# A diffusion trunk step on one core: conditioning products of 512 columns written as two of 256

## The reference

```python
def adaln(cvec, w, b):
    m = jax.nn.silu(cvec) @ w + b            # (groups, 1024) @ (1024, 6144) + (6144)
    return jnp.split(m[:, None, :], 6, axis=-1)

def trunk(x, cvec, ...):
    for l in range(DEPTH):                   # DEPTH = 2
        sh1, sc1, g1, sh2, sc2, g2 = adaln(cvec, ada_w[l], ada_b[l])
        h = rmsnorm(x, norm1_g[l]) * (1 + sc1) + sh1
        ...
        x = x + g1 * mix
        h = rmsnorm(x, norm2_g[l]) * (1 + sc2) + sh2
        ...
        x = x + g2 * ff
```

## Time and profile before

| what | value |
|---|---|
| median of 3 runs | 1561.68 us (1560.41 to 1563.05) |
| profiled execution, its own time | 1562.52 us |
| its span, first to last instruction | 1560.7 us |
| mean granted TensorE clock | 0.975 of full speed |
| TensorE (PE) busy, its weight loads (PEld) | 1496.6 us (96%), 1243.6 us (80%) |
| DVE, ACT, POOL busy | 1149.5 us (74%), 917.6 us (59%), 15.0 us (1%) |
| HBM read | 460.98 MB, 296 GB/s over the span |

### The profile page before, as it was taken

One profiled execution on the slowest core, in us unless ns is written; L12 is line 12 of the kernel. 1 busy time (PEld: TensorE's weight loads), 2 busy tenths in 40 slices (PEclk: granted clock), 3 DMA queues, 4 the chain that ended last, 5 costly groups with the idle time before them and its releaser, 6 DMA issues.

```text
span 1560.7 us, 21348 instructions
## 1 busy us (share of the span) xinstructions
PE 1496.6 (96%) x8173; PEld 1243.6 (80%) x8173; DVE 1149.5 (74%) x1054; ACT 917.6 (59%) x756; POOL 15.0 (1%) x28
## 2 busy tenths in 40 slices
PE   6999898999798999999999999999999999999997
PEld 3888796999577788888888878888888888887886
DVE  2658654555444788888888888878878888888886
ACT  1433442333313777677677677677767767766774
POOL 1000000000000000000000000000000000000000
PEclk9699999999998999999999999999999999999998
DMA  9758778655456799899899889989989989997990
GB/s 325 268 166 293 265 242 301 197 190 187 135 198 234 259 366 362 298 374 359 304 349 369 325 328 370 356 291 364 370 288 364 367 327 326 360 368 283 372 348 29
DMA packets 221825, 463.37 MB, mean 297 GB/s; under 512 B 7572, under 2 KB 48696, under 8 KB 221768
## 3 DMA queue, kind: packets, MB, share of 16 engines
q1 hardware_dynamic: 220984, 460.83, 81.8%
q0 software_dynamic: 784, 1.75, 0.5%
HBM read 460.98 MB, written 1.57 MB: 296 GB/s over the span
## 4 chain that ended last, share of the span: by engine, by line
PE 90%; DVE 3%; ACT 3%; DMA 2%; SPq 1%; issue 0%; POOL 0%; DVEq 0%; ACTq 0%
PE ps L409 87%; PE ps L790 2%; SPq L881 1%; ACT hT L978 1%; DMA raw<-in_w_in 1%; DVE w_lo L1133 1%; DMA raw<-in_fourier_w 1%; ACT w_hi L953 1%; DMA raw<-in_ffn_w 1%; DVE rstd L1208 1%; PE ps L447 0%; PE ps L487 0%; ACT arena L1090 0%; DVE xT L1366 0%; DVE hT L1212 0%
## 5 line engine op out<-in xcount | busy, mean ns | idle before, releaser
L409 PE MATMUL ps<-w_hi,rnd 128*128 128x512 f32 x2720 | 875.2, 398 | 1.6 <-DVE rnd L1442 1.6
L1448 DVE TENSOR_TENSOR w_lo<-raw,w_hi 128x2048 fp32r<-128x2048 f32 x335 | 765.3, 2290 | 144.7 <-ACT w_hi L1047 144.2
L1047 ACT ACTIVATE w_hi<-raw 128x2048 fp32r<-128x2048 f32 x336 | 644.0, 1918 | 201.8 <-PE ps L409 201.8
L409 PEld LDWEIGHTS ps<-w_hi,rnd 128*128 128x128 f32 x2720 | 511.1, 188 | 122.0 <-issue 1.8
L409 PE MATMUL ps<-w_lo,rnd 128*128 128x512 f32 x1360 | 537.6, 395 | 0.0
L409 PE MATMUL ps<-rnd,w_hi 128*128 128x256 f32 x1632 | 298.8, 286 | 8.7 <-DVE rnd L1219 6.8
L409 PEld LDWEIGHTS ps<-w_lo,rnd 128*128 128x128 f32 x1360 | 255.8, 188 | 57.9
L409 PEld LDWEIGHTS ps<-rnd,w_hi 128*128 128x128 f32 x1632 | 255.1, 193 | 16.3 <-issue 10.1
L409 PE MATMUL ps<-rnd,w_lo 128*128 128x256 f32 x816 | 231.5, 284 | 0.0
L1133 DVE TENSOR_TENSOR w_lo<-raw,w_hi 128x2048 fp32r<-128x2048 f32 x53 | 121.4, 2292 | 119.0 <-ACT w_hi L953 118.9
L953 ACT ACTIVATE w_hi<-raw 128x2048 fp32r<-128x2048 f32 x53 | 101.3, 1912 | 171.3 <-PE ps L409 109.3
(11 more groups left out here) (126 smaller groups left out, 557.9 us busy)
## 6 DMA issues: line engine op xcount, KB each, us to landing
raw<-in_moe_w SPq DMA_DIRECT2D x336, 1024.0 KB, 5.2
raw<-in_ada_w SPq DMA_DIRECT2D x48, 1024.0 KB, 7.1
raw<-in_ffn_w SPq DMA_DIRECT2D x33, 1024.0 KB, 5.4
raw<-in_w_in SPq DMA_DIRECT2D x12, 1024.0 KB, 11.5
raw<-in_w_out SPq DMA_DIRECT2D x4, 1024.0 KB, 8.2
raw<-in_fourier_w SPq DMA_DIRECT2D x4, 1024.0 KB, 7.4
out<-tok SPq DMA_DIRECT2D x4, 256.0 KB, 2.0
arena<-dft_constants POOLq DMA_DIRECT2D x1, 640.0 KB, 7.1
```

The source lines that it names most:

```text
L409: return pe.matmul(out, lhsT, rhs, start=first, stop=last, **kw)
L1047: act.activation(w_hi[:, slot, :], raw[:, m % RAW, :], ACT.Copy).then_inc(hi_done, 1)
L1448: dve.tensor_tensor(w_lo[:, slot, :], raw[:, m % RAW, :], w_hi[:, slot, :].bitcast(F32), ALU.subtract).then_inc(lo_done, 1)
```

## The change

In `ada_products`, each product of 512 columns is written as two of 256: a loop over two column halves `n` stands around the loop over the four strips, so a half of the weights is taken as four strips by the left 256 columns, then four strips by the right 256. The bank, the strips, the stationary operands and the signals are the same. The flag that starts a new sum is given by the first column half alone, and the builder's check of accumulation groups is told to pass over these products.

```diff
--- before.py
+++ after.py
@@ -429,9 +429,11 @@
                 if part == 0:
                     wholes[0] += 1
                 w = whole_weights(f"ada{l}", (mm_done, signals[0] + 1) if part else (whole_used, wholes[0]))
-                for k in range(STRIPS):
-                    last = mm(b[STRIP * k:STRIP * (k + 1)], cond[:, STRIPS * part + k, :], w[:, k, :], part == 0,
-                              part == 1)
+                for n in range(2):
+                    sl = slice(n * COLS // 2, (n + 1) * COLS // 2)
+                    for k in range(STRIPS):
+                        last = mm(b[STRIP * k:STRIP * (k + 1), sl], cond[:, STRIPS * part + k, :], w[:, k, sl],
+                                  part == 0 and n == 0, part == 1, skip_group_check=True)
                 if part == 0:
                     last.then_inc(whole_used, 1)
             done(last)
```

## The result

The changed kernel took 1570.23 us, the median of five runs (1564.69 to 1572.11), against 1562.05 us for the kernel before on the same chip: a ratio of 1.0049, 95% interval 1.0032 to 1.0065. By the medians it is 8.2 us slower, outside the forecast range. Twelve more runs of the changed kernel gave 1568.54 against 1562.64 us, 1.0034 [1.0017, 1.0051], 5.9 us.

A forecast was written before the change was run, and what follows sets the result against it. TensorE's matmuls hold 90% of the chain, and a conditioning wave is bound by its streaming columns. 11.5 units x 0.016 us add 0.18, the rest set at nothing: 1561.9 us, range 1559.3 to 1564.6.

The forecast's parts named there:

- The waves, the unit, the count: Conditioning products: 768 matmuls of 0.38 us, 768 loads of 0.11, loads in fours every 0.216 us, units of 1.93 to 1.94.
- The term of 11.5 x 0.016 = 0.18 us: Two 256-column waves against one of 512 cost 0.004 us more, 0.016 per unit, over the 11.5 units on the chain.
- The units that the chain holds: Eleven and a half of 24 conditioning units lie on the chain, the same after the change; the others run beside something longer.
- the cover of 0.14 us at the norm's sum: Thinnest cover of an off-chain unit, at 403.51 us: growth beyond 0.14 us would begin to show there.
- That the issue of a pair adds to the streaming: Rival in TensorE's sequence: 16 more pairs cost 0.93 us per unit, 10.7 us over 11.5 units, 1572.6 us; chance 0.05.
- strips out of step: Rival: a unit's 32 matmuls run one by one, 6.9 us per unit, 60 us more, 1622 us and above; chance 0.02.
- The sentence of the Trainium skill: Some 60 cycles per matmul, estimated 25 ns: 0.4 us per unit, 4.6 us in all, 1566.5 us; taken as hidden.
- "0.08 us of DMA time, in a stretch where loads end the chain only in part": Fetching 768 added instructions, 31 bytes each, 24 KB at 297 GB/s, costs 0.08 us of DMA time; set at nothing.
- "Waits, signals, DMAs and buffers stay where they were": In every unit, one signal after each half's last matmul as before, so the wave cost is the only term.
- The clock: Rival at TensorE's low stretches: one unit faster or slower, 1560.8 or 1563.0 us; beyond 0.2%, chance 0.04 gain, 0.01 loss.
- "would have to come from the clock's low stretches": Sign for the whole kernel: a difference above 1.5 us with units of 1.93 us comes from TensorE's low clock.

The follow-up runs named there:

- h3: The changed kernel, all 24 units split, plus 48 one-column matmuls between the halves of unit 3 in the prologue: 1561.36 us, 0.9994.
- c2: The changed kernel word for word, run a second time: 1568.54 us, 1.0034 to the kernel before.
- c4: The kernel before with only the first four units (prologue) split in two: 1563.05 us, 0.9998.
- h1: The kernel before, no product split, plus 24 one-column matmuls between the halves of unit 3 in the prologue: 1563.75 us, 1.0007.
- i2: The kernel before with 24 one-column matmuls in the prologue, the same as h1, run once more: 1562.88 us, 1.0002.
- c3: The changed kernel with its two loops exchanged, both column halves of a strip and then the next strip: 1572.33 us, 1.0055.
- f2: The kernel before with only the last eight units (layer 1, units 4 to 11) split: 1566.38 us, 1.0028.
- g1: The kernel before, no product split, plus 24 one-column matmuls behind unit 5 of layer 1, ahead of the Fourier mix: 1564.09 us, 1.0008.
- g2: The kernel before with the last eight units split, plus 48 one-column matmuls ahead of the Fourier mix: 1562.72 us, 1.0008.
- g3: The kernel before with only the FFN's five units split, plus 24 one-column matmuls ahead of the Fourier mix: 1561.86 us, 0.9997.
- g4: The kernel before with only the first eleven units split, plus 40 one-column matmuls ahead of the Fourier mix: 1562.44 us, 1.0001.
- h2: The kernel before, no product split, plus 40 one-column matmuls between the halves of unit 3 in the prologue: 1564.67 us, 1.0014.
- f4: The changed kernel plus 48 one-column matmuls behind unit 5 of layer 1, ahead of the Fourier mix: 1565.01 us, 1.0013.

## Why the prediction was wrong

**The waves, the unit, the count: right.** 768 matmuls of 0.38 us and 768 loads of 0.11 were forecast, and 0.379 and 0.110 came; a unit of 1.93 to 1.94 us, and 1.93 came. The term of 11.5 x 0.016 = 0.18 us is of the right size: 11.5 x 0.01 = 0.12 us by the rows of after, and h3 with everything split is within 0.2% of before. The units that the chain holds, and the cover of 0.14 us at the norm's sum, are as forecast; there the sum still starts 0.14 us behind the unit's end (402.63 + 1.93 = 404.56, 404.70).

**The rivals.** That the issue of a pair adds to the streaming would have made units of 2.85 us, and strips out of step of 6.9; neither came. The sentence of the Trainium skill ("TensorEngine Tiling (Array Packing)", Performance Considerations) on 60 cycles per matmul, read as a cost that each added matmul brings, is not borne out for these waves: 16 more matmuls on a unit cost 0.01 us, not 0.4.

**The step that failed: "0.08 us of DMA time, in a stretch where loads end the chain only in part".** The added instructions' fetch was priced as bytes over a bandwidth. The bytes were off by a factor of two: 31 bytes per instruction came from dividing one queue's total by the instructions of all engines, though that queue follows TensorE's stream and the trace has none of its packets over half of the span (621 to 1417 us in before). The runs show 256 instructions to a packet of 16,384 bytes, 64 each. But that is not what failed: three packets more (768 / 256; the pages count 43 in after and 40 in the earlier trace rows, each with the long gap) are still nothing as bandwidth. What counts is the place. Adding 576 instructions ahead of the Fourier mix, and 32 more with each unit inside it, moved the packets that were due anyway, from the free time between two loads (26.9 us behind the first product) onto both of them (13.5 and 39.8 us). A packet that took 0.9 to 2.0 us held back the load that it met by 0.5 to 1.9 us, and both of these loads are on the chain. With it fell "Waits, signals, DMAs and buffers stay where they were": instruction packets are DMA transfers too, and they moved. I counted how many packets come, and did not ask for each of them what it comes beside.

**The clock.** The prediction said that a difference above 1.5 us with units of 1.93 us "would have to come from the clock's low stretches". The units did take 1.93 us, but the clock is only a part of it: of the 4.06 us in the first profile of after 1.70 go with a low stretch of 3.4 us, and 2.36 are the two loads. In the second profile 1.92 + 1.19 are the loads, and low stretches behind the second and the third load go with the rest of 6.44. The clock mostly followed the loads. Behind a second load that was held back it was low in five profiles of eight (after, c2, c4, h1, i2; TensorE had waited 2.82 to 3.95 us), behind a third one in four of five. But in c3, f2 and g1 it stayed high behind the second load after waits of 2.92 to 3.52 us, and in g2 it fell after 2.44 with no load late. So the longer wait alone does not decide it, and why the clock falls in one execution and not in another is not shown.

**What the runs show, and what they leave open.** Shown: with the packets moved off the loads the changed kernel costs nothing (h3), and neither do parts of the change (g3, g4); with the last eight units alone, and both loads met, 3.8 us of it are there, and in the profile a stage as long as that of after (f2). Shown in the profiles without any split: with a packet beside either load that load takes 0.8 to 1.6 us longer than in before (h1, g1, i2, h2). Not shown: an unsplit kernel with both loads met at once, so that the whole 6 us appear without the split; the two loads met singly reached 0.4 to 2.7 us, inside the noise. The stages in the two profiles of after are 4.1 and 6.4 us longer, where the medians lost 8.2 and 5.9; of the executions without a profile no more is known. The 2.4 us of f4, with no load held back, are not explained. How a packet holds back a load on the DMA engines is not in the traces. The 1.5 to 2.4 us of the first sixteen units, seen twice, with intervals that begin at 1.0001 and 1.0003, have no cause that is shown: the same units in two parts, and all of them in h3, cost nothing, and the late start in their profiles stands in profiles of unsplit kernels as well.

No version beat the kernel before: h3 and g3, the fastest, are within their intervals of it.

## What to carry to other kernels

A change that only adds instructions can move every later instruction packet of that engine, so ask which transfers on the chain the moved packets will lie beside, and not only how many bytes they add. When a change costs a few microseconds and its own rows show nothing, compare the two traces stage by stage between fixed instructions, and look at the instruction queue inside the time of each load that grew. A few harmless instructions in an early wait, enough to complete a packet, tell a cost of the edit from a cost of its place; put them far from the stretch that you compare, and compare it without the products whose clock differs from execution to execution.

## What was not expected of the hardware

The products of rounded operands ran at one of two beats, a whole stretch at a time. The 1200 matmuls of 256 columns in the FFN, on the chain of g4, where no unit between them is split, against the earlier trace rows:

```profile
257.03 141.62 PE ps L409 x1200
```

141.62 us against 140.28, both at the full clock: some 117.8 or 116.7 ns apiece through the whole of it. Four of the twenty profiled executions had the slower beat over these 1200 products, four more over a shorter stretch of the FFN. It costs 1.3 us where it falls, and I found nothing in the kernel that chooses it.

The low clock behind the norm was also not the same from execution to execution of one kernel: around the first Fourier products before had two low stretches of 3.4 us, and before run again one of 13.7.
